# The gate maps of the second lookup: one rounded product of two parts instead of one float32 product

## The reference

```python
    sv, si = lax.top_k(s, PEER_TOPK)              # s: scores of 8 heads x 2 sets of 128 keys
    cand = (sv[:, :, 0, :, None] + sv[:, :, 1, None, :]).reshape(T, PEER_HEADS, PEER_TOPK * PEER_TOPK)
    fv, fi = lax.top_k(cand, PEER_TOPK)
    i1 = jnp.take_along_axis(si[:, :, 0], fi // PEER_TOPK, axis=-1)
    i2 = jnp.take_along_axis(si[:, :, 1], fi % PEER_TOPK, axis=-1)
    idx = (i1 * PEER_NKEYS + i2).reshape(T, PEER_HEADS * PEER_TOPK)
    g = jax.nn.softmax(fv, axis=-1).reshape(T, PEER_HEADS * PEER_TOPK)
    ...
        ue = u[ic]
        ve = v[ic]
        act = jax.nn.gelu(jnp.einsum('td,ted->te', hc, ue), approximate=False)
        return jnp.einsum('te,ted->td', gc * act, ve)
```

## Time and profile before

| | us |
|---|---|
| median of 3 runs | 4288.0 (4281.71 to 4290.5) |
| the profiled execution, its own time | 4285.34 |
| its span in the profile | 4283.5 |
| TensorE busy, of the span | 4176.2 (97%) |
| VectorE busy | 3066.2 (72%) |
| ScalarE busy | 1783.5 (42%) |
| GpSimd busy | 1372.6 (32%) |
| mean granted clock of TensorE | 0.993 |

### The profile page before, as it was taken

The page is one execution under the profiler, slowest core; times in us unless marked ns, Lnnn a source line. Parts: engine busy times, 40 slices in busy tenths (PEclk is TensorE's granted clock), DMA queues, the critical chain, the costliest instruction groups (busy, mean ns, idle before and its releaser), DMA issues.

```text
span 4283.5 us, 61359 instructions
## 1 busy us (share of the span) xinstructions
PE 4176.2 (97%) x24253; PEld 3718.2 (87%) x24253; DVE 3066.2 (72%) x4913; ACT 1783.5 (42%) x2960; POOL 1372.6 (32%) x737
## 2 busy tenths in 40 slices
PE   7999999999999999999999999999999999999999
PEld 5888778888888799867999999999999799998887
DVE  5775558877887676565599897798887675554676
ACT  3233352233233544263334776333334545444444
POOL 0000200000000100000378666777772158444443
PEclk9999999999999999999999999999999999999999
DMA  7543215544555365212477899999994166778885
GB/s 276 221 165 146 84 41 206 222 179 189 219 198 201 111 248 190 79 40 79 140 251 243 299 340 340 362 364 354 356 356 171 60 204 215 229 245 280 282 286 180
DMA packets 286589, 926.85 MB, mean 216 GB/s; under 512 B 19680, under 2 KB 170336, under 8 KB 212192
## 3 DMA queue, kind: packets, MB, share of 16 engines
q1 hardware_dynamic: 249440, 788.70, 51.8%
q0 software_dynamic: 36864, 134.23, 8.8%
HBM read 837.92 MB, written 84.93 MB: 215 GB/s over the span
## 4 chain that ended last, share of the span: by engine, by line
PE 82%; DVE 8%; DMA 4%; ACT 3%; POOL 1%; issue 1%; SPq 0%; ACTq 0%; POOLq 0%; DVEq 0%
PE bank L1148 23%; PE bank L1150 23%; PE bank L1149 23%; PE bank L1597 2%; DMA gates<-work 2%; DVE work L2726 1%; PE bank L1352 1%; PE bank L1143 1%; PE bank L1138 1%; PE bank L1134 1%; PE bank L1364 1%; POOL weight_ring_low L3025 1%; PE bank L1389 1%; DVE weight_ring_low L2307 1%; DMA work<-in_up_rows,work 1%
## 5 line engine op out<-in xcount | busy, mean ns | idle before, releaser
L3025 POOL TENSOR_TENSOR weight_ring_low<-weight_ring,up_high 128x1024 fp32r<-128x1024 f32 x233 | 587.8, 2528 | 454.3 <-ACT up_high L2055 453.0
L1150 PE MATMUL bank<-peer_h_high,weight_ring_low 128*128 128x256 f32 (+2 forms) x2240 | 698.4, 312 | 0.0
L1148 PE MATMUL bank<-peer_h_high,up_high 128*128 128x384 f32 (+1 forms) x2048 | 643.1, 314 | 16.4 <-POOL weight_ring_low L3025 8.2
L1149 PE MATMUL bank<-h_low,up_high 128*128 128x384 f32 (+1 forms) x2048 | 633.8, 309 | 0.0
L2142 ACT ACTIVATE down_high<-weight_ring 128x1024 fp32r<-128x1024 f32 x256 | 257.1, 1052 | 524.9 <-PE bank L1150 524.9
L1150 PE MATMUL bank<-h_high,weight_ring_low 128*128 128x512 f32 (+1 forms) x1280 | 464.5, 363 | 0.0
L2953 POOL TENSOR_SCALAR h<-work,params 128x256 f32<-128x256 f32 x12 | 11.8, 997 | 1377.0 <-PE bank L1504 874.8
L1148 PE MATMUL bank<-h_high,in_high 128*128 128x512 f32 (+1 forms) x1216 | 441.7, 363 | 0.4
L1149 PE MATMUL bank<-h_low,in_high 128*128 128x512 f32 (+1 forms) x1216 | 441.4, 363 | 0.0
L1150 PEld LDWEIGHTS bank<-peer_h_high,weight_ring_low 128*128 128x128 f32 x2240 | 425.8, 190 | 3.8
L2753 DVE TENSOR_TENSOR weight_ring_low<-weight_ring,down_high 128x1024 fp32r<-128x1024 f32 x128 | 309.0, 2414 | 161.2 <-ACT down_high L2142 161.2
(11 more groups left out here) (432 smaller groups left out, 10093.0 us busy)
## 6 DMA issues: line engine op xcount, KB each, us to landing
weight_ring<-in_up SPq DMA_DIRECT2D x128, 1024.0 KB, 5.6
weight_ring<-in_down SPq DMA_DIRECT2D x128, 1024.0 KB, 6.8
weight_ring<-in_mod_w SPq DMA_DIRECT2D x112, 1024.0 KB, 5.1
weight_ring<-in_ffn_in SPq DMA_DIRECT2D x88, 1024.0 KB, 7.0
weight_ring<-in_ffn_out SPq DMA_DIRECT2D x64, 704.0 KB, 5.0
gates<-work SPq DMA_DIRECT2D x40, 1024.0 KB, 9.9
gelu<-work SPq DMA_DIRECT2D x64, 384.0 KB, 7.0
work<-gates SPq DMA_DIRECT2D x32, 768.0 KB, 13.0
```

The source lines that it names most:

```text
L1148: mm(dst, w_high, a_high, start=first, stop=False)
L1149: mm(dst, w_high, a_low, start=False, stop=False)
L1150: return mm(dst, w_low, a_high, start=False, stop=last)
L3025: G.tensor_tensor(ring_low[:, slot, w], ring[:, slot, w], up_high[:, n % 3, :].bitcast(F32), ALU.subtract)\
```

## The change

Only for `l == 1`:

- The gates of all tokens are parted once into a rounded part `gate_high` (in SBUF) and the rest `gate_low` (in PSUM, beside `turn_iota`).
- For each half VectorE writes the second-key marks in the rounded form (`mark_rows`) and the first-key marks unweighted into one of two areas that hold eight pairs of 128 columns (`mark_pairs`, in the context columns of `peer_h_high` and `h_low`, which are not used there). GpSimd multiplies by the high gates into the first 128 columns of each pair (`high_marks`); then VectorE multiplies by the low gates in place (`low_marks`).
- TensorE makes a token's map by one product of 256 columns: high part and low part of the map side by side. The maps of one half take all four banks.
- ScalarE copies the high part to the gate tile (`begin_gates`), and VectorE adds the low part from PSUM (`join_gates`).
- VectorE makes marks two halves ahead. GpSimd's `high_marks` are put behind the splits of the first (or second, for half 0) and the third unit of a block.

```diff
+        mark_rows = high_low("mark_rows", [P, 2, SUB, P], work_at, 2 * SUB * P)
+        gate_high, gate_low = high_low("gate_high", [P, TL], work_at)[:, :], ps[TURN_BANK][:, 0:TL]
+        mark_pairs = [part[:, :, TL:T].rearrange("p t (a k) -> p t a k", a=2) for part in (peer_h_high, h_low)]
+        def half_gates(q, e):
+            k0 = q % 2 * SUB + 2 * e
+            parts = ps[KEY_BANK + e][:, :].rearrange("p (t a k) -> p a k t", a=2, k=P)
+            return gate_tiles[1][:, q // 2 % 2, :, k0:k0 + 2], (parts[:, 0], parts[:, 1])
...
                     pe.wait_ge(marks_weighted, 2 * g0 + q + 1)
+                    if l == 1:
+                        for c in range(2):
+                            wait_for(pe, gates_copied, 4 * g0 + 2 * (q - 1) + c + 1)
+                            for k in range(4 * c, 4 * c + 4):
+                                i = mm(ps[KEY_BANK + k // 2][:, k % 2 * TL:k % 2 * TL + TL], mark_rows[:, q % 2, k],
+                                       mark_pairs[q % 2][:, k].rearrange("p a k -> p (a k)"), start=True, stop=True)
+                            i.then_inc(gates_done, 1)
+                        return
...
+                def begin_gates(q):
+                    if q % 2 == 0:
+                        wait_for(act, gates_stored[q // 2 % 2], 16 * (g0 // 2 + q // 4))
+                    for c in range(2):
+                        act.wait_ge(gates_done, 4 * g0 + 2 * q + c + 1)
+                        for e in range(2):
+                            dst, (high, low) = half_gates(q, 2 * c + e)
+                            i = A(dst, high, ACT.Copy)
+                        i.then_inc(gates_begun, 1)
...
-                        copy_gates(q)
+                        if l == 0:
+                            copy_gates(q)
+                        else:
+                            begin_gates(q)
...
-                    V.tensor_tensor(second_mark[:, q % 2], every, spread(routed[:, 1, tokens], 2, P), ALU.is_equal)
-                    first = first_mark[:, q % 2]
+                    V.tensor_tensor((second_mark if l == 0 else mark_rows)[:, q % 2], every, spread(routed[:, 1, tokens], 2, P), ALU.is_equal)
+                    first = first_mark[:, q % 2] if l == 0 else mark_pairs[q % 2][:, :, 1]
                     V.tensor_tensor(first, every, spread(routed[:, 0, tokens], 2, P), ALU.is_equal).then_inc(marks_ready, 1)
-                    if l == 0:
-                        return
-                    dve.wait_ge(marks_ready, 2 * g0 + q + 1)
-                    V.tensor_tensor(first, first, spread(routed[:, 2, tokens], 2, P), ALU.mult).then_inc(marks_weighted, 1)
+                def part_gates():
+                    link(V.tensor_copy(gate_high, routed[:, 2, LAT]))
+                    subtract(gate_low, routed[:, 2, LAT], gate_high).then_inc(gates_parted, 1)
+                def low_marks(q):
+                    dve.wait_ge(gates_parted, 1)
+                    dve.wait_ge(marks_high, q + 1)
+                    low = mark_pairs[q % 2][:, :, 1]
+                    V.tensor_tensor(low, low.bitcast(F32), spread(gate_low[:, q * SUB:q * SUB + SUB], 2, P), ALU.mult).then_inc(marks_weighted, 1)
+                def join_gates(q):
+                    for c in range(2):
+                        dve.wait_ge(gates_begun, 2 * q + c + 1)
+                        for e in range(2):
+                            dst, (high, low) = half_gates(q, 2 * c + e)
+                            o = V.tensor_tensor(dst, dst, low, ALU.add)
+                        o.then_inc(gates_copied, 1)
...
+                if l == 1:
+                    part_gates()
                 marks(0)
+                if l == 1:
+                    marks(1)
+                    low_marks(0)
+                    split_up(split_beside(l)[0])
+                    low_marks(1)
                 for q in range(2 * blocks):
-                    if q + 1 < 2 * blocks:
+                    if l == 0 and q + 1 < 2 * blocks:
                         marks(q + 1)
-                    if l == 1 and q % 2 == 0:
-                        split_up(split_beside(l)[q // 2])
+                    if l == 1:
+                        if q + 2 < 2 * blocks:
+                            marks(q + 2)
+                        join_gates(q)
+                        if q % 2 and q + 1 < 2 * blocks:
+                            split_up(split_beside(l)[(q + 1) // 2])
+                        if q + 2 < 2 * blocks:
+                            low_marks(q + 2)
...
+                gates = routing_units(l)[1]
+                mark_behind = {gates[q // 2][2 * (q % 2) + (q == 0)]: q for q in range(2 * len(gates))} if l == 1 else {}
+                def high_marks(q):
+                    g0 = b0 * DENSE[0] // BLOCK
+                    pool.wait_ge(marks_ready, 2 * g0 + q + 1)
+                    pool.wait_ge(gates_parted, 1)
+                    pair = mark_pairs[q % 2]
+                    G.tensor_tensor(pair[:, :, 0], pair[:, :, 1].bitcast(F32), spread(gate_high[:, q * SUB:q * SUB + SUB].bitcast(F32), 2, P), ALU.mult)\
+                        .then_inc(marks_high, 1)
...
+                    if n in mark_behind:
+                        high_marks(mark_behind[n])
```

More of the change, by code:

```diff
@@ L502, in build @@
         softmax_in, softmax_out, routed_copied = sem("softmax_in"), sem("softmax_out"), sem("routed_copied")
-        marks_ready, marks_weighted = sem("marks_ready"), sem("marks_weighted")
+        marks_ready, marks_weighted, marks_high = sem("marks_ready"), sem("marks_weighted"), sem("marks_high")
+        gates_begun, gates_parted = sem("gates_begun"), sem("gates_parted")
         gates_done, gates_copied = sem("gates_done"), sem("gates_copied")
@@ L700, in build @@
         first_mark, second_mark = take(2, SUB, P), take(2, SUB, P)
+        mark_rows = high_low("mark_rows", [P, 2, SUB, P], work_at, 2 * SUB * P)
+        gate_high, gate_low = high_low("gate_high", [P, TL], work_at)[:, :], ps[TURN_BANK][:, 0:TL]
+        mark_pairs = [part[:, :, TL:T].rearrange("p t (a k) -> p t a k", a=2) for part in (peer_h_high, h_low)]
+        assert SUB == KC and TL == 2 * P
         gate_tiles = {1: take(2, NKEYS, BLOCK)}
```

## The result

| | median us | runs |
|---|---|---|
| before | 4286.66 (4281.71 to 4290.5) | 4 |
| changed | 4258.14 (4255.65 to 4265.62) | 4 |

The ratio is 0.994, with a 95% interval of 0.9929 to 0.9952: 0.5 to 0.7% faster, 21 to 30 us. Forecast were 4276.0 and 4261 to 4288. The direction was right, the size was not: the gain is more than twice the 10.7 us that 4276.0 means against this median, and the time lies under the range. A later run of the same kernel gave 4260.83, again 0.994 (0.9922 to 0.9958).

What follows compares the result with a forecast made beforehand. TensorE was taken as the bound of the gate stretch, 15.08 us a block; a VectorE-GpSimd ring of 14.26 would gain 11.4, less 0.5 behind it: -10.9, giving 4274.4 or 4277.1. Forecast 4276.0, range 4261 to 4288.

Steps and rivals of the forecast that it cites:

- I take 2.40: Price in us of one GpSimd upper mark (multiplying first-key marks by high gates), taken from splits; ends 2.3 and 3.35.
- the ring: VectorE and GpSimd waiting on each other in the gate stretch: 14.26 us a block, over TensorE's 13.44; chance 0.52.
- the first of the signs of being wrong: Forecast called itself wrong if GpSimd's marks take another time than the splits.
- the stretch: Part where the second lookup makes its gate maps, 15.08 us a block before; forecast gain there 11.4 us.
- The forecast's case with TensorE as the bound: Rival for the gate stretch: exclusion doesn't bite or VectorE's split finds a pause; 13.44 us a block, 4263; chance 0.17.
- Exclusion of VectorE's split and GpSimd, and none with an input in PSUM: In the gate stretch, two-SBUF-input VectorE work and GpSimd's add up, the split's 1.07 us included; PSUM-input operations run free.
- TensorE: Gate products: eight rounded ones of 256 columns take 0.96 us for 1.79; a block 13.44 us if it stayed the bound.
- The rivals: Other outcomes: TensorE stays the bound (first, 0.17), dearer marks or costlier tail (0.22), slower (0.09); also clock and DMA.
- Dearer marks: Rival: upper marks at 2.7 us each shrink the gain to about 2 us, 4285; chance 0.22 with a costlier tail.
- Behind the stretch: Later gate store and read-back before the down stage: 0.5 us added, ends 0 and 2; nothing after changes.
- The clock: Rival: TensorE's clock falls after the two starting waits, costing 2 us each time; held not to happen; no chance given.

Runs made afterwards that it cites:

- b0_after: The changed kernel itself, no edit, run again for comparison: 4260.83 us, ratio 0.994 to the kernel before.
- a1_dense: Changed kernel, GpSimd's upper marks reading a second input without repeats in place of the gates, each repeated 128 times: 4269.84 us, ratio 0.9971.
- a2_dense_free: Changed kernel, upper marks' second input without repeats, and VectorE's split subtracting a row from PSUM so it is not held: 4258.68 us, ratio 0.9943.
- a4_low_sbuf: Changed kernel with the lower gates in SBUF in place of PSUM: 4305.83 us, ratio 1.0053.
- a3_twice: Changed kernel with each of the eight rounded gate products of a half made twice: 4290.7 us, ratio 1.0014.
- b2_marks_twice: Changed kernel with GpSimd making each upper mark twice, one after the other: 4314.25 us, ratio 1.007.
- a7_start: Changed kernel, VectorE making the upper marks of half 0, and its lower marks ahead of the marks of half 1: 4259.84 us, ratio 0.9939.
- b1_start2: Changed kernel, VectorE making half 0's upper and lower marks first, GpSimd holding the third unit's split until gates are parted: 4263.59 us, ratio 0.9951.

## Why the prediction was wrong

The step that failed is one term of the sum: "I take 2.40" for the upper marks, with 2.3 as the lower end. It is 1.90. I wrote that no row has this operation with a repeated input, set the lower end a tenth below the splits, and took the value of the splits. No row of before spoke for so narrow an end. The upper marks lie twice in the ring: with 1.90 the forecast's own sum is 13.26 (measured 13.07), under TensorE's 13.44, and so TensorE stays the bound. That a mark takes another time than a split is the first of the signs of being wrong that the forecast named.

That term explains the stretch. The forecast's case with TensorE as the bound has the second product end at 3664.1, 15 blocks of 13.44 behind it, and 4263 in total. In the profile the second product ended at 3662.46, and 15 blocks of 13.44 later, at 3864.05, the last one: the 24.1 us that the stretch gained, in both executions of the changed kernel.

It doesn't explain all of the total. 4258.14 is 5 us below that 4263, and the forecast's lower end of 4261 lies between the two. In the profiled pair 5.6 of the 29.7 us were gained outside the stretch, of which 4.1 behind it; b0_after, with the same stretch, has 4260.83 as its median, and its span is only 23.0 us below that of before. So how far the time fell below the range owes something to what differs between executions.

- *The ring*: right. With marks of 2.41 (a1_dense) the kernel is 0.29% faster, 12.4 us, where 11.4 from the ring and 0.5 back were forecast; the block is 14.08 for 14.26. The error of 0.18 is of durations summed in place of starts. It did no harm by itself.
- *Exclusion of VectorE's split and GpSimd, and none with an input in PSUM*: right (a2_dense_free, a4_low_sbuf).
- *TensorE*: 0.96 us a product and 13.44 a block: right, to the hundredth (a3_twice).
- *The rivals*: the outcome is that of the first, TensorE stays the bound, but not for its reason. It was to come from VectorE's split finding a pause; the split is held as ever. A rival "the marks are cheaper" was missing. By the forecast's own sum TensorE binds from 1.99 us a mark down ((14.26 - 13.44) / 2 is 0.41 under 2.40), by the starts of a1_dense from 2.09.
- *Dearer marks*: did not happen. b2_marks_twice shows that what a mark costs counts in full once the ring binds: two more marks of 1.9 us in each round take it from 13.07 to 16.93.
- *GPSIMD Engine Reference, section Elementwise*, of the Trainium skill led to an estimate of 2.25 us for a two-input operation of this size. The splits are above it (2.41) and the marks below (1.90); it does not speak of a repeated input.
- *Behind the stretch*: no change forecast but 0.5 us; the profiled pair shows 4.1 us gained there. The wait before the first down product was 5.83 before and 1.75 in the changed kernel's profile, but 3.27 in b0_after, which is the same kernel. In the other edits it was 3.3 to 6.0. So this is a difference of executions as much as of kernels; what part the change has in it stays open.
- *The clock*: I held that it would not fall at the start. In the profiled execution it did: the first product behind the wait of 2.16 us took 2.08 us, and the granted clock of the stretch 3650 to 3655 was 0.79. In b0_after, with the same wait, the product took 1.22 and the clock stayed at 1.00. It cost nothing here: in b0_after TensorE waited 1.11 us before the second product instead, and from the first product to the third it is 15.0 us in both.

TensorE in order of time at the first product, in the changed kernel and in b0_after:

```profile
3653.06 2.08 PE L1608 MATMUL bank<-peer_h_high,mark_rows 128*128 128x256 f32 x8 [2.16 <-DVE peer_h_high L2889]
```

```profile
3657.24 1.22 PE L1608 MATMUL bank<-peer_h_high,mark_rows 128*128 128x256 f32 x8 [2.16 <-DVE peer_h_high L2889]
```

## What to carry to other kernels

Where two engines hand work to each other, busy shares don't tell whether they fit: write down one round of who waits for whom and add up the starts, with what they exclude each other from. From 3700 to 3850 us GpSimd was busy for 91% in the version that lost 12 us (a1_dense) and for 89% in the one that lost nothing (a2_dense_free). Then ask of each price in the round from which value on it changes what binds (here 1.99 for a guess of 2.40). If no row shows the operation itself, its nearest relative alone must not set the lower end, and if that value can't be excluded, both outcomes need a chance.

## What the runs showed of the hardware

- A GpSimd product of 128x1024, rounded out, takes 1.90 us if its second input is eight elements, each repeated 128 times, and 2.41 if it is 1024 elements read one after the other (a1_dense).
- A VectorE operation with two SBUF inputs and one of GpSimd exclude each other for whole instructions, and it goes both ways (a1_dense): the VectorE subtraction waits to the end of GpSimd's operation (3.36 us for 1.2), and a GpSimd split behind it takes 3.40 for 2.4.
- GpSimd's work also holds a VectorE copy of 128x256 float32 with its one input and its output in SBUF: 2.23 us (a7_start) for 0.29 (b1_start2). The Trainium skill, GPSIMD Engine Reference, section Key points, names two-port modes beside two inputs; that a copy with one input is held agrees with it, though no row shows the mode of the copy.
- The small joinings with an input in PSUM were never held (405 to 426 ns each of 128 in the changed kernel, beside GpSimd at 82%).
